# A hybrid attention and gMLP layer on one core: q and k projected by seven products of token halves and k halves

## The chip, the cores and the metric

The kernel runs on one core of a Trainium2 chip. Times are microseconds on the device, from the first to the last instruction of one execution; the metric is the median over repeated runs. Engines: TensorE (PE, with its weight loads PEld), VectorE (DVE), ScalarE (ACT), GpSimd (POOL) and SyncE (SP), which issues most DMAs.

## What is computed

One decoder layer on 512 tokens of width 1024. A single input projection feeds attention (8 heads of 64, rotary on the first 16 dimensions, causal, with blocks of 256 of which all earlier ones are chosen at this size) and a gated spatial mixing (gMLP). Both results are normalised, joined and projected, then come a squared-ReLU MLP of width 4096 and a gated per-layer embedding. All is fp32.

```python
hn = rms_norm(h, mix_pre_g[i])
proj = jnp.einsum('bsd,de->bse', hn, w_in[i])
q, k, v, u, gv = jnp.split(proj, [D_ATTN, 2 * D_ATTN, 3 * D_ATTN, 3 * D_ATTN + D_GMLP], axis=-1)
q = partial_rope(q.reshape(B, S, N_ATTN_HEADS, HEAD_DIM), pos)
k = partial_rope(k.reshape(B, S, N_ATTN_HEADS, HEAD_DIM), pos)
attn_out = moba_attention(q, k, v)
gmlp_out = gmlp_spatial_gating(gelu(u), gelu(gv), ...)
mixed = concatenate([rms_norm(attn_out, ...), rms_norm(gmlp_out, ...)])
h = h + rms_norm(mixed @ w_o[i], mix_post_g[i])
```

## The kernel before

**Split numbers.** Every fp32 matrix is written as a high part (rounded to fp32r by ScalarE) and a low part (the remainder, by VectorE). `product` then does three matmuls into one bank: high by high, high by low, low by high.

**Input projection.** x comes in transposed (`xT_raw`, 16 KB a partition) and is split into `actT_hi` and `actT_lo`. The weights come as slabs of 128 rows by 512 columns; SyncE loads them in pairs into `raw` (four places), ScalarE multiplies by the norm gain and writes `w_hi`, VectorE writes `w_lo` (`splits`). A ring of 16 places holds two groups of eight slabs. A tile `("proj", n)` is 128 tokens by 512 columns: 8 slabs by 3 matmuls, 24 matmuls of 128x512. The groups in order are gv (0 to 3), u (4 to 7), q (8 to 11), k (12 to 15), v (16 to 19); proj 20 to 27 are the output projection.

**Around it.** `normalise` on GpSimd and `ln_centre` on VectorE alternate over the four token tiles of gv: GpSimd computes a root, VectorE centres, GpSimd applies gain and offset. Then GpSimd masks the mixing weights. `mix(i)` does the spatial mixing of two channel groups, `mix_drain(i)` multiplies u by it. q and k tiles are scaled into `work` (two places) by ScalarE, rotated there by GpSimd (`rotate`, five small operations) and transposed by TensorE (`turn_qk`, result `qkT`); ScalarE and VectorE drain the transposes into high and low parts. `turn_gate` does the same with the mixed u. `scores(0)` is the first work of attention, and proj 17 comes behind it.

**Order.** Each engine runs its own list of instructions as the code is written; semaphores are the only link between engines. `phase_one_results` names the order in which banks of PSUM are filled and which bank each result uses; `bank_free` makes TensorE wait until the last user of a bank is drained. SyncE's list is in order as well: a load that waits for its place holds up those behind it. Proj 17 and everything behind it are the same in both kernels, but for places named below.

Of the kernel before, what the change touches and what calls it, by code (L numbers as in the profile page):

```python
# [166 lines left out]
def phase_one_results():  # L167
# [26 lines left out]
    return names[:names.index(("proj", 17))] + [name for name, _ in late], banks  # L194
# [43 lines left out]
EARLY_SPLITS = (KD, KD + 2, KD + 4, KD + 6, KD + 8)  # L238
SPLIT_AT = {n: KD + 2 * (n + 1) for n in range(TT, 16)}


def hymba_layer(nc, x, xT, pT, weights, columns, rope, ws, rows, out):
# [6 lines left out]
    with ExitStack() as ctx:  # L249
# [29 lines left out]
        top[0] = -(-top[0] // (2 * KIB)) * 2 * KIB  # L279
        h = place("h", [P, TT, D])  # L280
# [49 lines left out]

        acc = place("acc", [P, TT, D], at=at_area)
# [11 lines left out]
        at_h = 20 * KIB  # L343
# [49 lines left out]
        rstd_ln = stat[:, 80:84]  # L393
        bn6 = lambda t: stat[:, 90 + 6 * t:96 + 6 * t]
# [28 lines left out]
        roped = sem("roped")  # L423
        gm_squared, gm_rstd, gm_scaled = sem("gm_squared"), sem("gm_rstd"), sem("gm_scaled")
# [73 lines left out]
        drained = {}  # L498

# [87 lines left out]
        def _(dve):  # L587
# [85 lines left out]
            def qkT_lo(i):  # L673

                cut = slice(i % TT * P, (i % TT + 1) * P)
                high, low = ((qT_hi, qT_lo), (kT_hi, kT_lo))[i // TT]
                if i == TT:
                    dve.wait_ge(xT_lo_done, len(X_PIECES))
# [16 lines left out]
            splits(EARLY_SPLITS[4])  # L695
            for n in range(TT, 16):
                if n in SPLIT_AT:
                    splits(SPLIT_AT[n])
                if n in (TT, TT + 1):
                    ln_centre(n - 2)  # L700
                if n in (9, 10):
                    mix_drain(2 * (n - 9))
                    mix_drain(2 * (n - 9) + 1)
                if n >= 10:
                    qkT_lo(n - 10)
                if n == 11:
                    dve.wait_ge(gm_rstd, 1)
                    for t in range(TT):
                        nc.vector.tensor_scalar(u[:, t, :], u[:, t, :], rstd_gm[:, t:t + 1], None,
                                                ALU.mult).then_inc(gm_scaled, 1)  # L710
# [1871 lines left out]
```

## Time and profile before

| what | value |
|---|---|
| median of 3 runs | 590.27 us (589.64 to 590.51) |
| the profiled execution: time, span | 589.68 us, 588.0 us |
| TensorE busy | 579.6 us (99%) |
| VectorE busy | 467.4 us (79%) |
| ScalarE busy | 340.0 us (58%) |
| GpSimd busy | 100.7 us (17%) |
| mean granted clock of TensorE | 0.997 |

Busy shares are means over the whole span. A matmul's record lasts longer than the distance to the next one, since matmuls are pipelined; the pace is read from the distance between starts. In a timeline a row gives the start, the time from there to the end of the last of its instructions, and in brackets how long the engine sat idle before it and what released it.

### The profile page before, as it was taken

What the parts mean: (1) busy time and instruction counts of PE and PEld (TensorE: products, weight loads), DVE (VectorE), ACT (ScalarE), POOL (GpSimd) and SP (SyncE); (2) the same over time, 40 slices, a digit from 0 to 9 for tenths busy, and PEclk for the clock granted to TensorE, in tenths of its full rate; (3) what the DMA queues carried; (4) which work ended last, traced back from release to release, by engine and by line L of the source; (5) the groups of instructions that cost most, each with busy time, mean ns of one, the idle gap of its engine ahead of it and who ended that gap; (6) DMA issues with size and microseconds to landing.
All of it is one profiled execution on the core that took longest, in us unless ns stands there. A gap on an engine that the chain in (4) does not pass through costs nothing.

```text
span 588.0 us, 8944 instructions
## 1 busy us (share of the span) xinstructions
PE 579.6 (99%) x3424; PEld 505.5 (86%) x3424; DVE 467.4 (79%) x623; ACT 340.0 (58%) x555; POOL 100.7 (17%) x159
## 2 busy tenths in 40 slices
PE   9999999999999999999999999999999999999995
PEld 7888888888888878888999989999999999988885
DVE  5655554567866999899999989999999899799655
ACT  6835535657554746676565565764656657654422
POOL 0166333000112445001101010011010100001011
PEclk9999999999999999999999999999999999999998
DMA  8945332112203368649478394583773845584011
GB/s 272 337 130 182 124 107 73 36 64 82 72 1 109 112 246 295 135 112 269 75 226 179 72 268 90 150 245 55 241 168 75 261 96 137 207 292 190 0 73 71
DMA packets 25673, 87.16 MB, mean 148 GB/s; under 512 B 2976, under 2 KB 4384, under 8 KB 25120
## 3 DMA queue, kind: packets, MB, share of 16 engines
q1 hardware_dynamic: 19872, 64.50, 32.3%
q0 software_dynamic: 4032, 14.68, 14.4%
q10 hardware_dynamic: 1728, 7.42, 3.4%
q8 instruction: 27, 0.44, 0.3%
q14 instruction: 14, 0.11, 0.1%
HBM read 80.30 MB, written 6.29 MB: 147 GB/s over the span
## 4 chain that ended last, share of the span: by engine, by line
PE 87%; DVE 5%; DMA 4%; ACT 2%; issue 1%; SPq 0%; POOL 0%; ACTq 0%; DVEq 0%
PE psum L2082 27%; PE psum L2086 27%; PE psum L2087 27%; DMA ple_spill<-ple 2%; PE psum L2137 2%; PE psum L2269 2%; PE psum L2249 1%; DMA raw<-weights_dram 1%; DVE up_lo L832 1%; PE psum L2151 1%; DVE w_lo L600 1%; DMA first_raw_a<-weights_dram 1%; ACT t_hi L1581 1%; DVE raw L957 1%; DVE acc L1032 0%
## 5 line engine op out<-in xcount | busy, mean ns | idle before, releaser
L2082 PE MATMUL psum<-w_hi,actT_hi 128*128 128x512 f32 (+1 forms) x230 | 89.5, 389 | 0.0
L2087 PE MATMUL psum<-w_hi,actT_lo 128*128 128x512 f32 (+1 forms) x230 | 88.0, 383 | 0.0
L2086 PE MATMUL psum<-w_lo,actT_hi 128*128 128x512 f32 (+1 forms) x230 | 87.8, 382 | 0.0
L2082 PE MATMUL psum<-t_hi,a_hi 128*128 128x512 f32 x216 | 84.8, 393 | 0.3 <-DVE acc L1030 0.3
L2086 PE MATMUL psum<-t_lo,a_hi 128*128 128x512 f32 x216 | 84.6, 392 | 0.0
L2087 PE MATMUL psum<-t_hi,a_lo 128*128 128x512 f32 x216 | 84.0, 389 | 0.0
L2087 PE MATMUL psum<-sum_hi,up_lo 128*128 128x256 f32 x224 | 63.4, 283 | 0.0
L2086 PE MATMUL psum<-sum_lo,up_hi 128*128 128x256 f32 x224 | 63.4, 283 | 0.0
L2082 PE MATMUL psum<-sum_hi,up_hi 128*128 128x256 f32 x224 | 63.2, 282 | 0.0
L2087 PE MATMUL psum<-actT_hi,up_lo 128*128 128x256 f32 (+1 forms) x200 | 60.0, 300 | 0.0
L2086 PE MATMUL psum<-actT_lo,up_hi 128*128 128x256 f32 (+1 forms) x200 | 60.0, 300 | 0.0
L2082 PE MATMUL psum<-actT_hi,up_hi 128*128 128x256 f32 (+1 forms) x200 | 59.9, 299 | 0.0
L1903 POOL DMA_DIRECT2D raw_x<-weights_dram x21 | 18.5, 883 | 213.0 <-DVE t_lo L975 212.7
L603 DVE SCALAR_TENSOR_TENSOR w_lo<-raw,cols,w_hi 128x512 fp32r<-128x512 f32 x48 | 38.2, 838 | 18.7 <-ACT w_hi L1234 18.7
L2087 PEld LDWEIGHTS psum<-w_hi,actT_lo 128*128 128x128 f32 x230 | 43.2, 188 | 8.4
L1034 DVE TENSOR_TENSOR acc<-acc,psum 128x512 f32<-128x512 f32 x76 | 49.0, 680 | 1.8 <-PE psum L2087 1.8
L2082 PEld LDWEIGHTS psum<-w_hi,actT_hi 128*128 128x128 f32 x230 | 43.3, 188 | 8.3
L2086 PEld LDWEIGHTS psum<-w_lo,actT_hi 128*128 128x128 f32 x230 | 43.3, 188 | 8.0
L832 DVE TENSOR_TENSOR up_lo<-raw,up_hi 128x1024 fp32r<-128x1024 f32 x37 | 46.7, 1262 | 3.4 <-ACT up_hi L1447 2.8
L2087 PEld LDWEIGHTS psum<-t_hi,a_lo 128*128 128x128 f32 x216 | 40.6, 188 | 8.9
L2082 PEld LDWEIGHTS psum<-t_hi,a_hi 128*128 128x128 f32 x216 | 40.8, 189 | 7.7 <-issue 0.5
L2086 PEld LDWEIGHTS psum<-t_lo,a_hi 128*128 128x128 f32 x216 | 40.7, 189 | 6.6
(229 smaller groups left out, 1337.0 us busy)
## 6 DMA issues: line engine op xcount, KB each, us to landing
raw<-weights_dram SPq DMA_DIRECT2D x42, 512.0 KB, 3.5
raw_o<-weights_dram SPq DMA_DIRECT2D x23, 512.0 KB, 4.4
raw_x<-weights_dram POOLq DMA_DIRECT2D x21, 512.0 KB, 5.6
raw_second<-weights_dram SPq DMA_DIRECT2D x14, 512.0 KB, 4.2
raw_x<-weights_dram SPq DMA_DIRECT2D x9, 512.0 KB, 6.1
gate_raw<-weights_dram SPq DMA_DIRECT2D x8, 512.0 KB, 4.8
raw_o<-weights_dram POOLq DMA_DIRECT2D x7, 512.0 KB, 7.6
h<-x_dram ACTq DMA_DIRECT2D x4, 512.0 KB, 4.8
```

Source lines behind the costliest of these rows:

```text
L600: nc.vector.tensor_tensor(w_lo[:, place_at, :], source, high, ALU.subtract).then_inc(slab_lo, 1)
L603: nc.vector.scalar_tensor_tensor(out=w_lo[:, place_at, :], in0=source, scalar=gain, in1=high, op0=ALU.mult, op1=ALU.subtract).then_inc(sla ...
L832: nc.vector.tensor_tensor(up_lo[q % UP_SLOTS][:], block_source(step, j), up_hi[q % UP_SLOTS][:].bitcast(F32), ALU.subtract).then_inc(block ...
L957: nc.vector.tensor_tensor(target, target, block, ALU.add).then_inc(block_summed, 1)
L1034: nc.vector.tensor_tensor(part, part, bank, how).then_inc(product_added, 1)
L1581: nc.scalar.activation(t_hi[n % T_RING][:], t_source(n), ACT.Copy).then_inc(t_hi_done, 1)
L1903: nc.gpsimd.dma_start(raw_x[step % 2][:], weights[down_in_stream(step, rows, half)], accum_op=ALU.add).then_inc(x_added, 16)
L2082: begin = nc.tensor.matmul(out, a_hi, b_hi, start=first, stop=False, skip_group_check=read_between)
L2086: nc.tensor.matmul(out, a_hi, b_lo, start=False, stop=False, skip_group_check=read_between)
L2087: return nc.tensor.matmul(out, a_lo, b_hi, start=False, stop=last, skip_group_check=read_between)
L2137: mm = nc.tensor.transpose(psum[:, banks[name], j * P:(j + 1) * P], source[:, j * P:(j + 1) * P], ident[:])
L2269: mm = nc.tensor.matmul(psum[s * DH:(s + 1) * DH, BANK_O, pair * P:(pair + 1) * P], v[:, k, head * DH:(head + 1) * DH], probsT_of[place_in ...
```

## The change

q and k are computed together as a 2 by 2 block product. With X the tokens in halves by k in halves (X11, X12; X21, X22) and W the k halves by the columns of q and of k (W11, W12; W21, W22), seven products of sums replace the eight plain ones. A product is two token tiles by four k slabs by three matmuls, 24 matmuls of 128x512. The names BLOCK_21, BLOCK_11, BLOCK_T1, BLOCK_T2, BLOCK_T3, BLOCK_22, BLOCK_T4 give the weight block or sum of each product, in order; SUM_E, SUM_S2, SUM_S3, SUM_S4 are the sums of x halves.

- The four weight blocks are loaded whole (2 DMAs of 512 KB each) into `qk_raw`, gained in place by ScalarE (`qk_gain`, four operations of 128x512 each), and split whole, 128x2048 (`qk_split_hi`, `qk_split_lo`). T1, T2 and T4 are summed in the place of block 11, T3 in that of block 12 (`qk_sum_blocks`).
- The sums of x are made in `xT_raw`, and split into `xs_hi` and `xs_lo`, which lie where x was in `h`. So x is loaded again by SyncE, after product 22.
- Results are put together by ScalarE copies (`qk_copies`) and VectorE (`qk_sum`), with a negated rstd that GpSimd now makes. The q and k tiles come out as q0, q1, k2, k3, k0, k1, q2, q3.
- `mix(0)` and `mix(1)` stand behind product 21, `mix(2)` and `mix(3)` behind product 11, in banks 4 and 7 by turns. proj 16 (v, tile 0) is split around two transposes, and the transposes of q2 and q3 stand behind proj 17.

```diff
+QK_ORDER = ((QK_Q, 0), (QK_Q, 1), (QK_K, 2), (QK_K, 3), (QK_K, 0), (QK_K, 1), (QK_Q, 2), (QK_Q, 3))
...
+    for i in range(4):
+        banks["mix", i] = (BANK_S + 1, BANK_O)[i % 2]
...
+        qk_raw = {BLOCK_21: place("qk_raw_21", [P, 4, W], at=at_second_raw),
+                  BLOCK_11: place("qk_raw_11", [P, 4, W], at=at_area + 16 * KIB),
+                  BLOCK_T3: place("qk_raw_12", [P, 4, W], at=at_mixed_hi),
+                  BLOCK_22: place("qk_raw_22", [P, 4, W], at=at_mixed_lo)}
...
+            def qk_split_lo(j):
+                dve.wait_ge(qk_hi, j + 1)
+                high, low = qk_places(j)
+                nc.vector.tensor_tensor(low, qk_source(j)[:], high.bitcast(F32), ALU.subtract).then_inc(qk_lo, 1)
...
+                nc.vector.tensor_tensor(target[:], target[:], block[:], ALU.add).then_inc(qk_blocks_summed, 1)
...
+            xs_sum(SUM_E, x_block(1, 0), x_block(1, 1), ALU.subtract, 1)
+            ln_centre(2)
+            ln_centre(3)
+            qk_split_lo(BLOCK_21)
...
+            xs_sum(SUM_S4, x_block(0, 1), xs_source(SUM_S2), ALU.add, 4)
+            qk_sum_blocks(BLOCK_T1)
+            xs_split_lo(SUM_S2)
+            qk_split_lo(BLOCK_T1)
+            qk_sum_blocks(BLOCK_T2)
+            qk_split_lo(BLOCK_T2)
+            qk_sum_blocks(BLOCK_T3)
+            mix_drain(0)
+            mix_drain(1)
...
+            nc.gpsimd.tensor_scalar(neg_rstd_x, rstd_x, -1.0, None, ALU.mult).then_inc(x_rstd, 1)
...
+            sp.wait_ge(qk_filled, 2 * BLOCK_22 + 2)
+            for t in range(TT):
+                sp.dma_start(h[:, t, :], x[t * P:(t + 1) * P]).then_inc(x_loaded[t], 16)
...
+            qk_product(BLOCK_21)
+            mix(0)
+            mix(1)
+            qk_product(BLOCK_11)
+            mix(2)
+            mix(3)
+            qk_product(BLOCK_T1)
+            turn_qk(0)
+            turn_qk(1)
+            qk_product(BLOCK_T2)
+            qk_product(BLOCK_T3)
+            turn_gate(0)
+            qk_product(BLOCK_22)
```

VectorE before, from the splits of the last u slabs and the first q slabs (`w_lo`) with the centrings (`gv`) to the drains of the mixing groups (`u`):

```order
L603 SCALAR_TENSOR_TENSOR w_lo<-raw,cols,w_hi 128x512 [waits slab_hi] x4
L655 TENSOR_SCALAR gv<-gv,stat 128x512 [waits ln_rstd]
L603 SCALAR_TENSOR_TENSOR w_lo<-raw,cols,w_hi 128x512 [waits slab_hi] x2
L655 TENSOR_SCALAR gv<-gv,stat 128x512 [waits ln_rstd]
L603 SCALAR_TENSOR_TENSOR w_lo<-raw,cols,w_hi 128x512 [waits slab_hi] x8
L668 SCALAR_TENSOR_TENSOR u<-psum,cols,u 128x4x64 [waits act_drained,filled]
L668 SCALAR_TENSOR_TENSOR u<-psum,cols,u 128x4x64
L668 SCALAR_TENSOR_TENSOR u<-psum,cols,u 128x4x64 [waits filled]
L668 SCALAR_TENSOR_TENSOR u<-psum,cols,u 128x4x64
```

VectorE after, from the sum E to the same drains (`qk_raw_91` is block 21, `_92` block 11 and the sums in its place, `_93` block 12, `_94` block 22; `xs_lo_97` and `_98` are the two places of x sums):

```order
L729 TENSOR_TENSOR xT_raw<-xT_raw 128x2x512
L699 TENSOR_SCALAR gv<-gv,stat 128x512 [waits ln_rstd,xs_summed]
L699 TENSOR_SCALAR gv<-gv,stat 128x512 [waits ln_rstd]
L740 TENSOR_TENSOR w_lo<-qk_raw_91,w_hi 128x2048 [waits qk_hi]
L729 TENSOR_TENSOR xT_raw<-xT_raw 128x2x512
L729 TENSOR_TENSOR xT_raw<-xT_raw 128x2x512 [waits xs_summed]
```

and a little further on:

```order
L751 TENSOR_TENSOR qk_raw_92<-qk_raw_92,qk_raw_93 128x2048 [waits qk_gained,qk_lo,xs_summed]
L734 TENSOR_TENSOR xs_lo_98<-xT_raw,xs_hi_96 128x1024 [waits xs_hi_done]
L740 TENSOR_TENSOR w_lo<-qk_raw_92,w_hi 128x2048 [waits qk_hi]
L751 TENSOR_TENSOR qk_raw_92<-qk_raw_92,qk_raw_94 128x2048 [waits qk_gained,qk_lo]
L740 TENSOR_TENSOR w_lo<-qk_raw_92,w_hi 128x2048 [waits qk_hi]
L751 TENSOR_TENSOR qk_raw_93<-qk_raw_93,qk_raw_94 128x2048 [waits qk_gained,qk_blocks_summed]
L712 SCALAR_TENSOR_TENSOR u<-psum,cols,u 128x4x64 [waits act_drained,filled]
L712 SCALAR_TENSOR_TENSOR u<-psum,cols,u 128x4x64
L712 SCALAR_TENSOR_TENSOR u<-psum,cols,u 128x4x64 [waits filled]
L712 SCALAR_TENSOR_TENSOR u<-psum,cols,u 128x4x64
L740 TENSOR_TENSOR w_lo<-qk_raw_93,w_hi 128x2048 [waits qk_hi]
L760 SCALAR_TENSOR_TENSOR work<-psum,stat,work 128x512 [waits qk_filled,qk_copied] x2
```

The drains of mixing groups 0 and 1 stood behind plain splits; now they stand behind the block sums and low parts of T1 and T2 and the sum T3, each with a wait for ScalarE's high part, and no split is left between the centrings.

ScalarE before, from the drain of the second u tile (`u`) with the splits around it to the drain of the first q tile (`work`):

```order
L1307 ACTIVATE u<-psum,stat 128x512 [waits filled]
L1234 ACTIVATE w_hi<-raw,cols 128x512 [waits slab_used,raw_loaded1]
L1234 ACTIVATE w_hi<-raw,cols 128x512
L1349 DMA rope_sb<-rope_dram 128x128
L1307 ACTIVATE u<-psum,stat 128x512 [waits filled]
L1234 ACTIVATE w_hi<-raw,cols 128x512 [waits slab_used,raw_loaded0]
L1234 ACTIVATE w_hi<-raw,cols 128x512
L1307 ACTIVATE u<-psum,stat 128x512 [waits filled]
L1234 ACTIVATE w_hi<-raw,cols 128x512 [waits slab_used,raw_loaded1]
L1234 ACTIVATE w_hi<-raw,cols 128x512
L1312 ACTIVATE work<-psum,stat 128x512 [waits filled]
```

ScalarE after, from the drain of the u tile of proj 6 on (`work` now holds the copies of product 21):

```order
L1436 ACTIVATE u<-psum,stat 128x512 [waits filled]
L1451 ACTIVATE qk_raw_94<-qk_raw_94,cols 128x512 [waits qk_raw_loaded3]
L1451 ACTIVATE qk_raw_94<-qk_raw_94,cols 128x512 x3
L1464 ACTIVATE w_hi<-qk_raw_92 128x2048 [waits slab_used,qk_blocks_summed]
L1436 ACTIVATE u<-psum,stat 128x512 [waits filled]
L1464 ACTIVATE w_hi<-qk_raw_92 128x2048 [waits slab_used,qk_blocks_summed]
L1485 ACTIVATE work<-psum,stat 128x512 [waits qk_filled] x2
L1464 ACTIVATE w_hi<-qk_raw_93 128x2048 [waits qk_filled,qk_blocks_summed]
L1464 ACTIVATE w_hi<-qk_raw_94 128x2048 [waits qk_filled,qk_gained]
```

The drain of the last u tile, proj 7, has moved behind the high part of T1, and the copies of product 21 behind that of T2.

TensorE at mixing groups 2 and 3, before and then after (L2371 is `mix`, `xs_hi` marks product T1):

```order
L2151 MATMUL psum<-gv,wsT 128x256 [waits dve_drained]
L2151 MATMUL psum<-gv,wsT 128x256
L2151 MATMUL psum<-gv,wsT 128x256 [waits dve_drained]
L2151 MATMUL psum<-gv,wsT 128x256
L2137 MATMUL psum<-ident,work 128x128 [waits act_drained,roped]
```

```order
L2371 MATMUL psum<-gv,wsT 128x256 [waits dve_drained]
L2371 MATMUL psum<-gv,wsT 128x256
L2371 MATMUL psum<-gv,wsT 128x256 [waits dve_drained]
L2371 MATMUL psum<-gv,wsT 128x256
L2302 MATMUL psum<-w_hi,xs_hi_95 128x512 [waits qk_copied,xs_lo_done,qk_lo]
```

In both, groups 2 and 3 wait for VectorE to drain groups 0 and 1. Behind them stood the first transpose; now there is product T1, which waits for the copies of product 21, the low part of E and the low part of T1.

## Rows read from the trace of the kernel before

**Rows 1.** the page: busy times, and the clock in 40 slices

```profile
PE 579.6 (99%) x3424; PEld 505.5 (86%) x3424; DVE 467.4 (79%) x623; ACT 340.0 (58%) x555; POOL 100.7 (17%) x159
...
PEclk9999999999999999999999999999999999999998
```

**Rows 2.** the page: the chain that ended last, by engine

```profile
PE 87%; DVE 5%; DMA 4%; ACT 2%; issue 1%; SPq 0%; POOL 0%; ACTq 0%; DVEq 0%
```

**Rows 3.** timeline of TensorE: start us, us, engine, line, tiles, count

```profile
54.70 1.89 PE L2151 MATMUL psum<-gv,wsT 128*128 128x256 f32 x8
...
56.24 0.58 PE L2082 MATMUL psum<-w_hi,actT_hi 128*128 128x512 f32 x1
...
57.80 0.39 PE L2082 MATMUL psum<-w_hi,actT_hi 128*128 128x512 f32 x1
...
61.66 0.39 PE L2087 MATMUL psum<-w_hi,actT_lo 128*128 128x512 f32 x1
...
106.77 0.60 PE L2137 MATMUL psum<-ident,work 128*128 128x128 f32 x4
...
107.30 0.34 PE L2082 MATMUL psum<-kT_hi,mixT_hi 64*128 64x128 f32 x2
...
108.80 0.50 PE L2082 MATMUL psum<-w_hi,actT_hi 128*128 128x512 f32 x1
```

**Rows 4.** groups by form, VectorE: shapes, count, busy us, mean ns, idle before

```profile
L832 DVE TENSOR_TENSOR up_lo<-raw_second,up_hi 128x1024 fp32r<-128x1024 f32 x14 | 17.1, 1221 | 1.2 <-ACT up_hi L1447 0.5
...
L981 DVE TENSOR_TENSOR a_lo<-f,a_hi 128x512 fp32r<-128x512 f32 x28 | 19.1, 682 | 0.4 <-ACT a_hi L1592 0.4
...
L603 DVE SCALAR_TENSOR_TENSOR w_lo<-first_raw_b,cols,w_hi 128x512 fp32r<-128x512 f32 x4 | 2.8, 749 | 0.7 <-ACT w_hi L1234 0.7
```

**Rows 5.** timeline of ScalarE at 36.90

```profile
36.90 2.55 ACT L1234 ACTIVATE w_hi<-raw,cols 128x512 fp32r<-128x512 f32 x4
```

**Rows 6.** groups by form, ScalarE

```profile
L1447 ACT ACTIVATE up_hi<-raw_second 128x1024 fp32r<-128x1024 f32 x14 | 14.7, 1048 | 0.0
```

**Rows 7.** timeline of VectorE, 18 to 62

```profile
18.12 1.41 DVE L603 SCALAR_TENSOR_TENSOR w_lo<-raw,cols,w_hi 128x512 fp32r<-128x512 f32 x2 [0.70 <-ACT w_hi L1234]
...
29.05 2.44 DVE L603 SCALAR_TENSOR_TENSOR w_lo<-raw,cols,w_hi 128x512 fp32r<-128x512 f32 x2
...
48.03 0.55 DVE L655 TENSOR_SCALAR gv<-gv,stat 128x512 f32<-128x512 f32 x1 [0.44 <-POOL stat L1799]
...
59.85 1.65 DVE L668 SCALAR_TENSOR_TENSOR u<-psum,cols,u 128x256 f32<-128x256 f32 x4
```

**Rows 8.** timeline of GpSimd, 29 to 84

```profile
29.31 1.64 POOL L1819 TENSOR_TENSOR gv<-gv,ln_gb 128x512 f32<-128x512 f32 x1 [1.74 <-DVE gv L655]
...
37.92 1.29 POOL L1819 TENSOR_TENSOR gv<-gv,ln_gb 128x512 f32<-128x512 f32 x1 [0.72 <-DVE gv L655]
...
52.07 1.09 POOL L1832 TENSOR_SCALAR_AFFINE_SELECT wsT<-wsT 128x1024 f32<-128x1024 f32 x1
...
83.50 0.32 POOL L1848 TENSOR_TENSOR work<-rope_tmp 128x64 f32<-128x64 f32 x1
...
83.79 0.83 POOL L1850 TENSOR_TENSOR work<-rope_tmp 128x64 f32<-128x64 f32 x1
```

**Rows 9.** the page: DMA issues, KB, us to landing

```profile
raw<-weights_dram SPq DMA_DIRECT2D x42, 512.0 KB, 3.5
```

**Rows 10.** timeline of VectorE at the first scores

```profile
108.18 0.69 DVE L621 TENSOR_TENSOR kT_lo<-psum,kT_hi 128x512 fp32r<-128x512 f32 x1 [4.78 <-ACT kT_hi L1253]
...
108.92 1.23 DVE L722 TENSOR_TENSOR psum<-psum,causal 128x1024 f32<-128x1024 f32 x1
```

**Rows 11.** timeline of TensorE, the first turned probabilities

```profile
115.73 1.03 PE L2249 MATMUL psum<-ident,probs 128*128 128x128 f32 x8
```

**Rows 12.** windows at the end: TensorE busy (x), PEclk, DMA

```profile
581.00:582.00 1.00, 0.84 (x8) 0.63 (x6) 0.00 (x0) 0.12 (x1) 0.85 (x2) 1.00 0.00 0
...
585.00:585.50 0.50, 0.00 (x0) 0.00 (x0) 0.47 (x2) 0.00 (x0) 0.00 (x0) 0.50 0.00 0
```

More of the change, by code:

```diff
@@ L673, in qkT_lo @@
             def qkT_lo(i):
[L675 to L678, printed above, removed]
+                which, t = QK_ORDER[i]
+                cut = slice(t * P, (t + 1) * P)
+                high, low = ((qT_hi, qT_lo), (kT_hi, kT_lo))[which]
                 turn_lo(("qkT", i), low[:, :, cut], high[:, :, cut], bank1["qkT", i])
@@ L694, in _ @@
             ln_stats_of(3)
[L695 to L710, printed above, removed]
-                if 12 <= n <= 15:
-                    gate_turn_lo(n - 12)
@@ L716, in row_maxima @@
+            qkT_lo(2)
+            qkT_lo(3)
+            qk_sum(4)
+            qk_sum(5)
+            gate_turn_lo(1)
+            splits(G_V * KD + 4)
+            splits(G_V * KD + 6)
+            gate_turn_lo(2)
+            qkT_lo(4)
+            qkT_lo(5)
+            gate_turn_lo(3)
+            splits(G_O0 * KD)
             def row_maxima(unit):
@@ L1307, in proj_drain @@
                     last = nc.scalar.activation(u[:, t, :], bank, ACT.Gelu, scale=rstd)
-                elif group in (G_Q, G_K):
-                    i = n - 2 * TT
-                    if i >= 2:
-                        act.wait_ge(filled, filled1["qkT", i - 2])
-                    last = nc.scalar.activation(work[:, i % 2, :], bank, ACT.Copy, scale=rstd)
                 else:
@@ new lines, in _ @@
+            proj_drain(7)
+            qk_split_hi(BLOCK_T2)
+            qk_copies(BLOCK_21)
+            qk_split_hi(BLOCK_T3)
+            qk_split_hi(BLOCK_22)
+            act.wait_ge(*drained["mix", 3])
+            for t in range(TT):
+                square(u[:, t, :], ss_gm[:, t:t + 1], gm_squared)
+            qk_copies(BLOCK_T1)
+            qkT_hi(0)
+            qkT_hi(1)
+            xs_split_hi(SUM_S3)
+            qk_split_hi(BLOCK_T4)
+            qk_copies(BLOCK_T2)
+            xs_split_hi(SUM_S4)
@@ L1364, in _ @@
+            gate_turn_hi(0)
+            splits(G_V * KD)
+            splits(G_V * KD + 2)
+            qkT_hi(2)
+            qkT_hi(3)
+            gate_turn_hi(1)
+            splits(G_V * KD + 4)
+            splits(G_V * KD + 6)
+            qk_scale(6)
+            qk_scale(7)
+            gate_turn_hi(2)
+            act.wait_ge(qk_summed, 6)
+            act.dma_start(gain_post[:], rows["mix_post"]).then_inc(post_loaded, 16)
+            qkT_hi(4)
+            qkT_hi(5)
             proj_drain(16)
-            qkT_hi(7)
+            gate_turn_hi(3)
@@ L2224, in scores @@
+            proj(16, range(0, 4))
+            turn_qk(4)
+            turn_qk(5)
+            proj(16, range(4, KD))
+            turn_gate(3)
             def scores(unit):
```

309 lines of the change are left out of this document (239 added, 70 removed).

## The prediction

> **What bounds the kernel now.** I read the page's busy times and clock first [rows 1]: TensorE is busy for 99% of the span and its granted clock reads 9 (90% or more) in every slice but the last. The chain that ended last [rows 2] gives 87% to TensorE, 5% to VectorE and 4% to DMA. Then I read the stretch that changes in order of time [rows 3]. From the products of u to the first scores TensorE never stops: 18 matmuls lie between the starts at 57.80 and 61.66, less one, so 17 steps take 3.86 us, 0.227 each; a tile of 24 takes 5.45. The mixing block begins at 54.70, which is where the first q tile ends, so the u products end at 54.70 - 5.45 = 49.25. The v tile that follows the first scores (proj 17) starts at 108.80. The stretch is 59.55 us long and TensorE alone fills it. So a matmul less is worth 0.227 us, if its operands are there in time, and any wait of TensorE here goes straight to the end.
>
> **What the change takes away.** q and k took 8 tiles of 24 matmuls, now 7 products of 24: 5.45 us. Two transpose groups (qkT 6 and 7) go behind proj 17; one group takes 107.30 - 106.77 = 0.53 or less [rows 3], I take 0.48, so 0.96 leaves the stretch and comes back behind it.
>
> **What it adds.** On VectorE, 16 splits of 128x512 go (0.75 each [rows 4], 0.66 start to start). In come 4 sums of x halves and 4 low parts of them (128x1024), 4 sums of weight blocks and 7 low parts of blocks (128x2048), and 6 sums of results (128x512). A 1024-wide one takes 1.22 us and a 512-wide one 0.68 [rows 4], so 0.54 more for each further 512: 2048 wide is 2.30, and 2.26 start to start; 1024 is 1.14. That is 11 x 2.26 + 8 x 1.14 + 6 x 0.65 = 37.9 us for 10.6. On ScalarE, gaining four blocks is 16 x 0.64 (four take 2.55 [rows 5]); a 1024-wide copy is 1.05 [rows 6], so a 2048-wide is about 1.9, and 1.8 start to start. Each block has to go ScalarE (high), VectorE (low), VectorE (sum onto it), ScalarE (high) and so on, because T1 and T2 are summed in the place of block 11. That is the chain to follow.
>
> **The schedule, by these durations.** VectorE's fourth centring waited for GpSimd until 48.03 [rows 7] with splits just before it. Now the splits in front of it are gone, and it runs at about 47.5; VectorE can do nothing in between, since it stands ahead of the first low part. The low part of block 21 runs 47.9 to 50.2. TensorE was ready at 49.25: **wait 1.1**.
> GpSimd's last normalising (two operations of 1.3, each 1.29 when alone) and its mask of the mixing weights (1.09) come now [rows 8]. In the trace two splits next to such an operation took 2.44 in place of 1.41 [rows 7], and GpSimd's 1.64 in place of 1.29 [rows 8]: 29.31 + 1.64 = 30.95, and one more split after that ends at 31.5, just what one operation after another gives. So I let operations of VectorE with two inputs in SBUF and operations of GpSimd take turns, 3.6 us for VectorE here. The sums for S3 and S2 end at 55.0 and the low part of 11 at 58.3. TensorE has finished 21 and two mixing groups (56.24 - 54.70 = 1.54 [rows 3]) at 57.3: **wait 1.2**.
> Low part of E, sum S4, block sum T1 end at 63.0. ScalarE makes T1's high part until 64.9, and only behind it drains proj 7 (65.6), whose bank the second half of product 11 needs at 61.2: **wait 4.5**.
> Low T1 to 67.4, sum T2 to 69.8, high T2 on ScalarE to 71.7, low T2 to 74.1, sum T3 to 76.4, and then the drains of mixing groups 0 and 1 (four operations take 1.65 [rows 7], 0.83 a group). Mixing group 2 now reuses the bank of group 0, so TensorE, ready at 68.4, starts it at 77.3: **wait 8.9**.
> T1 runs 79.0 to 84.4. The two rotations on GpSimd begin at 81.5, while VectorE goes from mixing drains to the sum T4 and the low part of 22, 2.26 each. A small GpSimd operation took 0.83 in place of 0.32 next to one split of 0.75 [rows 8]; the second rotation gets one of its five operations in between each long one and ends at 89.2. TensorE has done the first transpose at 84.9: **wait 4.4**.
> T2 starts at 89.8; behind it I find no wait over 0.1 us up to proj 17: T3's x part is ready when T2 ends, and the v slabs (loads 3.5 us [rows 9]) and blocks are in time. The second load of x is 4 transfers on SyncE's queue when product 22 is done (about 105). It is wanted some 40 us later, and even if they land one after another, 14 us, the w_o slabs queued behind them land by 122.5 and are wanted at 123: 0. The negated rstd costs GpSimd 0.3 before it joins the first wait.
> Waits: 1.1 + 1.2 + 4.5 + 8.9 + 4.4 = 20.1. Proj 17 starts at 108.80 - 5.45 - 0.96 + 20.1 = 122.5, 13.7 later.
>
> **Behind it.** The transposes come back: +0.96. Before, the row maxima of the first scores began 0.12 after proj 17 (108.92) [rows 10]. Now a gate low part and two splits stand ahead of them on VectorE, 2.1 us behind proj 17, and two low parts stand ahead of the drain of the turned probabilities. TensorE turned the probabilities at 115.73 with 1.3 in hand [rows 11]; by the same arithmetic it now waits 1.2 for the inverse, 1.3 for the drain and 1.0 in the next group, 3.5 in all. The bounds are 0 (the cover that attention had, used up differently) and 3.5; I take 2.0. After that TensorE is as full as before and nothing gives the time back. **Sum: 13.7 + 1.0 + 2.0 = 16.7.** The profiled execution took 589.68 (span 588.0), so 606.4 by it; the median of the three runs is 0.6 higher, 590.27, so **607.0**.
>
> **Taking turns, or not.** The turn-taking above is read off the rows: 2.44 for 1.41. The Trainium skill ("SBUF — State Buffer", section "Who interferes with whom") says that an instruction of VectorE with two SBUF inputs and one of GpSimd that reads SBUF exclude each other, the first one keeping the ports to its end. The trace agrees, with 30.95 and 31.5. Without it the sum is that of the first rival.
>
> **The rivals.**
> 1. GpSimd hinders the long operations little (they overlap as far as they like). Then the waits are 2.3 (proj 7), 8.9 (mixing) and 2.3 (T3's x part), 13.5 together, and the sum 13.5 - 6.4 + 3.0 = 10.1: 600.4. The 8.9 stays, since no GpSimd work lies beside it. Against it: rows 7 and 8. Chance 0.17.
> 2. Clock. In the trace TensorE's last matmuls are in 581:582, at a clock of 1.00, and in 585:585.5, after 3 us without one, it reads 0.50 [rows 12]. A wait of 8.9 us outlasts that, and T1 would start at 1.2 GHz. If all 24 matmuls of T1 ran at twice 0.227 that is 5.45 more, but the wait of 4.4 behind T1 takes up most: +1. If T2 were slow too, +5.5 more: 612. Chance 0.08. The Trainium skill ("TensorE: Matmul & The Clock Gate", section "HAM oscillation — how this bites in real kernels") says that a long gap drops the clock again; the trace agrees on the fall at its end and shows no recovery inside the kernel.
> 3. The shift is partly taken back in attention and the layers after it, or the small waits are hidden: only the 8.9 and 2.3 at full size, and the rest half. 8.9 + 2.3 + 2.2 + 1.2 - 6.4 + 1.0 = 9.2: 599.5. For it: VectorE has gaps in this stretch, as the 4.78 before 108.18 [rows 10]. Chance 0.12.
> 4. Faster than before. One mechanism: the 2048-wide operations run at a higher rate than the shorter ones. The point from which it decides is about 0.6 us each on VectorE with 0.8 on ScalarE: then the waits before proj 17 are 2.3 and it starts 4.2 earlier; with all of the 3.5 behind it hidden, 1.0 of transposes back, the time is 587. Against it: 512 and 1024 wide are in proportion in the trace (0.68, 1.22). Chance 0.03.
> Forecast 0.60.
>
> **The numbers.** The likeliest case itself spans 14 to 19 more (2048 wide at 2.15 or 2.35 moves it by 1.4 either way, attention 0 or 3.5): 604 to 610. The range takes in rivals 1 to 3 up to their middles, for a chance left out of 2 in 10: 598 to 612. Within 0.2% (1.2 us, what a measurement of this kernel can tell from no change) lies only an accident between rivals 3 and 4: 0.02. Faster 0.03, slower 0.95.
>
> **What the profile will show.** TensorE busy falls from 99% to about 96%, with idle ahead of the mixing matmuls released by VectorE's u operations (near 68 to 77), ahead of a w_hi product released by ScalarE's u drain (near 61 to 66) and ahead of a transpose released by GpSimd (near 85 to 89). The 2048-wide operations read 2.3 (VectorE) and 1.9 (ScalarE). Proj 17 starts near 122. I am wrong if the drains of mixing groups 0 and 1 come before 70, if the long operations are shorter than 1.6, or if the second rotation ends less than 3 us after the first.

## The result, and the profile after

The changed kernel takes 605.14 us (median of 4 runs, 605.03 to 605.33), the kernel before 590.07 beside it on the same chip (589.64 to 590.51): a ratio of 1.0256, 95% interval 1.0238 to 1.0273. It is slower by 15.1 us; 16.7 were forecast, to 607.0. The profiled executions differ as much: span 603.1 against 588.0.

The page of the kernel after, busy times and slices, to be read beside [rows 1]:

```profile
span 603.1 us, 8912 instructions
...
PE 580.3 (96%) x3400; PEld 504.7 (84%) x3400; DVE 494.5 (82%) x632; ACT 356.8 (59%) x566; POOL 107.5 (18%) x160
...
PE   9999389999999999999999999999999999999995
...
DVE  5638887577867699799999999989999999789655
...
PEclk9999779999999999999999999999999999999999
...
PE 70%; DVE 12%; DMA 5%; ACT 5%; POOL 4%; issue 2%; SPq 1%; ACTq 0%; DVEq 0%; POOLq 0%
```

TensorE has a hole in the fifth and sixth slices (60 to 90 us), its clock falls in the same two, and the chain that ended last has lost 17 points of TensorE to the other engines [rows 2]. The timeline of TensorE from 49 to 122 us, cut to the steps that the prediction names, and at the end projection 17 (compare [rows 3]):

```profile
50.60 0.50 PE L2302 MATMUL psum<-w_hi,actT_hi 128*128 128x512 f32 x1 [0.68 <-DVE w_lo L740]
...
56.18 1.89 PE L2371 MATMUL psum<-gv,wsT 128*128 128x256 f32 x8
...
58.17 0.50 PE L2302 MATMUL psum<-w_hi,actT_hi 128*128 128x512 f32 x1
...
65.29 0.79 PE L2302 MATMUL psum<-w_hi,actT_hi 128*128 128x512 f32 x1 [4.10 <-ACT u L1436]
...
69.37 0.40 PE L2307 MATMUL psum<-w_hi,actT_lo 128*128 128x512 f32 x1
...
76.63 3.78 PE L2371 MATMUL psum<-gv,wsT 128*128 128x256 f32 x8 [6.86 <-DVE u L712]
79.85 0.99 PE L2302 MATMUL psum<-w_hi,xs_hi 128*128 128x512 f32 x1
...
86.58 0.60 PE L2357 MATMUL psum<-ident,work 128*128 128x128 f32 x4
...
88.48 0.66 PE L2357 MATMUL psum<-ident,work 128*128 128x128 f32 x4 [1.30 <-POOL work L2051]
...
121.47 0.51 PE L2302 MATMUL psum<-w_hi,actT_hi 128*128 128x512 f32 x1
```

The three longer waits are the three large ones of the forecast, each by the engine it named: ScalarE's drain of projection 7 (L1436) ahead of the second half of product 11, VectorE's drains of mix 0 and 1 (L712) ahead of mix 2, GpSimd's rotation (L2051) ahead of the second turn. Projection 17 starts 12.67 later than in [rows 3] (121.47 for 108.80).

ScalarE at the first of these waits: the high part of T1, and behind it the drain of projection 7.

```profile
62.75 1.91 ACT L1464 ACTIVATE w_hi<-qk_raw 128x2048 fp32r<-128x2048 f32 x1 [3.60 <-DVE qk_raw L751]
64.57 0.67 ACT L1436 ACTIVATE u<-psum,stat 128x512 f32<-128x512 f32 x1
```

VectorE and GpSimd in the same stretch, from their timelines (compare [rows 7, 8]):

```profile
48.26 2.29 DVE L740 TENSOR_TENSOR w_lo<-qk_raw,w_hi 128x2048 fp32r<-128x2048 f32 x1
50.46 4.56 DVE L729 TENSOR_TENSOR xT_raw<-xT_raw 128x1024 f32<-128x1024 f32 x2
55.05 3.07 DVE L740 TENSOR_TENSOR w_lo<-qk_raw,w_hi 128x2048 fp32r<-128x2048 f32 x1
...
75.70 1.66 DVE L712 SCALAR_TENSOR_TENSOR u<-psum,cols,u 128x256 f32<-128x256 f32 x4
```
```profile
48.49 3.21 POOL L2019 TENSOR_TENSOR gv<-gv,ln_gb 128x512 f32<-128x512 f32 x1 [0.73 <-DVE gv L699]
...
82.64 0.46 POOL L2046 TENSOR_TENSOR rope_tmp<-work,rope_sb 128x128 f32<-128x128 f32 x1
83.06 2.37 POOL L2047 TENSOR_TENSOR rope_tmp<-work,rope_sb 128x64 f32<-128x64 f32 x1
85.39 2.37 POOL L2048 TENSOR_TENSOR rope_tmp<-work,rope_sb 128x64 f32<-128x64 f32 x1
```

A 2048-wide operation takes 2.29 alone and 3.07 beside GpSimd; GpSimd's operation of 1.29 takes 3.21, and its operation of 0.32 takes 2.37 when a long one of VectorE has just begun. The clock, from the windows (columns: stretch, length, busy of PE, PEld, DVE, ACT, POOL, granted clock, DMA):

```profile
61.00:65.00 4.00, 0.19 (x1) 0.00 (x0) 3.16 (x3) 2.25 (x2) 0.00 (x0) 1.00 0.00 0
65.00:68.00 3.00, 2.71 (x6) 2.15 (x7) 2.97 (x2) 0.24 (x1) 0.00 (x0) 0.50 0.00 0
68.00:70.00 2.00, 1.76 (x7) 1.08 (x5) 1.31 (x1) 0.65 (x1) 0.00 (x0) 0.89 0.00 0
...
76.00:80.00 4.00, 3.37 (x9) 2.75 (x9) 3.59 (x6) 3.53 (x2) 0.00 (x0) 0.50 0.00 0
80.00:83.00 3.00, 3.00 (x10) 2.35 (x10) 3.00 (x8) 0.02 (x1) 1.98 (x6) 0.65 0.00 0
83.00:86.00 3.00, 3.00 (x15) 2.47 (x14) 3.00 (x2) 2.90 (x9) 3.00 (x3) 1.00 0.00 0
```

Already the wait of 4.1 us leaves TensorE at 0.50, 1.2 GHz, for most of the second half of product 11. After the wait of 6.9 all of the mixing and the first four matmuls of T1 run at it (a matmul then takes 0.43 us from start to start in place of 0.23).

### The profile page after: what moved, and what is told of

It is laid out like the page before. It is cut to its first block, busy times and chain, and to the rows that moved or that the text cites. A ratio compares the mean times of both kernels' runs of the same rounds, so it can differ in the third digit from the quotient of the medians.

```text
span 603.1 us, 8912 instructions
## 1 busy us (share of the span) xinstructions
PE 580.3 (96%) x3400; PEld 504.7 (84%) x3400; DVE 494.5 (82%) x632; ACT 356.8 (59%) x566; POOL 107.5 (18%) x160
## 4 chain that ended last, share of the span: by engine, by line
PE 70%; DVE 12%; DMA 5%; ACT 5%; POOL 4%; issue 2%; SPq 1%; ACTq 0%; DVEq 0%; POOLq 0%
PE psum L2302 22%; PE psum L2306 22%; PE psum L2307 22%; DMA ple_spill<-ple 2%; DMA raw<-weights_dram 2%; DVE up_lo L956 2%; PE psum L2541 2%; PE psum L2357 1%; PE psum L2521 1%; DVE w_lo L740 1%; DVE qk_raw L751 1%; DMA first_raw_b<-weights_dram 1%; ACT w_hi L1464 1%; DVE xT_raw L729 1%; DVE w_lo L647 1%
## 5 line engine op out<-in xcount | busy, mean ns | idle before, releaser
L2302 PE MATMUL psum<-w_hi,actT_hi 128*128 128x512 f32 (+1 forms) x190 | 74.4, 392 | 4.9 <-ACT u L1436 4.1
L2307 PE MATMUL psum<-w_hi,actT_lo 128*128 128x512 f32 (+1 forms) x190 | 72.9, 383 | 0.0
L2306 PE MATMUL psum<-w_lo,actT_hi 128*128 128x512 f32 (+1 forms) x190 | 72.8, 383 | 0.0
L2302 PEld LDWEIGHTS psum<-w_hi,actT_hi 128*128 128x128 f32 x190 | 36.1, 190 | 12.9 <-ACT u L1436 4.5
L2302 PEld LDWEIGHTS psum<-sum_hi,up_hi 128*128 128x128 f32 x224 | 42.9, 191 | 1.1
L2306 PEld LDWEIGHTS psum<-sum_lo,up_hi 128*128 128x128 f32 x224 | 42.9, 191 | 1.1
L2307 PEld LDWEIGHTS psum<-sum_hi,up_lo 128*128 128x128 f32 x224 | 42.9, 191 | 0.0
```

The costliest lines, as they stand in the source:

```text
L2302: begin = nc.tensor.matmul(out, a_hi, b_hi, start=first, stop=False, skip_group_check=read_between)
L2306: nc.tensor.matmul(out, a_hi, b_lo, start=False, stop=False, skip_group_check=read_between)
L2307: return nc.tensor.matmul(out, a_lo, b_hi, start=False, stop=last, skip_group_check=read_between)
```

## The experiments

All start from the changed kernel; runs 8 to 10 change the order of much of it. Each ratio is to the kernel before on the same chip; the changed kernel's is 1.0256. Theory A and theory B are those of the text on record ahead of each run.

**1. The drain of projection 7 first.** On ScalarE:

```diff
+            proj_drain(7)
             qk_split_hi(BLOCK_T1)
-            proj_drain(7)
```

> Only the order on ScalarE changes: the drain of projection 7 comes ahead of the high part of T1, so that the second half of product 11 no longer waits for it (4.1 us in the kernel after the change). Theory A, VectorE's row of long operations from 48 to 78 us sets when mix 2 may begin, whatever TensorE does before: the 4.1 us go over to the wait ahead of mix 2, which grows from 6.9 to about 11 us and still ends at 76.6, and the time stays within 0.5 us of 605.1. Theory B, each wait of TensorE is a cost of its own: the 4.1 us are saved, 601.0.

604.97 us, ratio 1.0255 (1.0241 to 1.0269). From its list of TensorE's steps:

```profile
76.61 3.78 PE L2371 MATMUL psum<-gv,wsT 128*128 128x256 f32 x8 [12.68 <-DVE u L712]
```

Theory A: 4.1 us are taken from one wait and stand in the next, with the 1.6 us that the half product no longer loses to the low clock, and that wait ends where it did (76.61 for 76.63). TensorE's waits here are not costs that add up; VectorE's row of operations sets the end.

**2. The drains of mix 0 and 1 first.** As 1, and on VectorE:

```diff
             xs_split_lo(SUM_S2)
+            mix_drain(0)
+            mix_drain(1)
             qk_split_lo(BLOCK_T1)
             ...
-            mix_drain(0)
-            mix_drain(1)
```

> As the run before, and on VectorE the drains of mix 0 and 1 come ahead of the low part of T1 in place of behind the sum of T3. Mix 2 then starts some 12 us sooner, at about 65. Theory A (VectorE's amount of work up to the rotated queries is the bound, not its order): what was won is lost again ahead of product T1 (the copies of product 21 and the low part of T1) and ahead of the two turns of the queries; the first turn is at 86 to 88 as before, and the time is 605 to 606.5. Theory B (the order of VectorE's work is at fault): the 6.9 us ahead of mix 2 are saved for the most part, 599 or less.

608.08 us, ratio 1.0314 (1.0300 to 1.0328). TensorE's three large waits in it, and the window behind the last:

```profile
72.44 0.77 PE L2302 MATMUL psum<-w_hi,xs_hi 128*128 128x512 f32 x1 [5.92 <-ACT work L1485]
...
83.06 0.66 PE L2357 MATMUL psum<-ident,work 128*128 128x128 f32 x4 [2.56 <-POOL work L2051]
...
88.92 1.12 PE L2357 MATMUL psum<-ident,work 128*128 128x128 f32 x4 [5.21 <-POOL work L2051]
```
```profile
89.00:95.00 6.00, 6.00 (x18) 4.86 (x19) 4.71 (x8) 3.34 (x3) 1.18 (x2) 0.54 0.02 4
```

Mix 2 starts at 64.5, 12 us sooner, and the second turn no sooner (88.92 for 88.48). That is theory A, but I missed the size by 1.6 us or more: the last wait is now 5.2 us, and the first 11 matmuls of product T2 behind it run at half speed (the mean clock from 89 to 95 is 0.54), so that T2 takes 7.8 us in place of 5.45. A wait that moves takes the drop of the clock with it, to a place where nothing covers it. That the order does not count holds for this exchange only: runs 8 to 10 put work before 48 us, and there it does.

**3. The two waits filled with work.** On TensorE, behind each half of product 11:

```diff
+                    if b == BLOCK_11:
+                        for _ in range((66, 115)[j]):
+                            nc.tensor.matmul(psum[:, BANK_PT, 0:P], warm[:], warm[:], start=True, stop=True)
```

> TensorE gets work that nobody needs in its two long waits: 66 matmuls of 128x128 behind the first half of product 11 and 115 behind the second half, at 0.053 us each at the full clock 3.5 and 6.1 us, a little less than the waits of 4.1 and 6.9 us. If idling is what lets the granted clock fall, it stays at 1.00 from 61 to 86 us, mixing takes 1.6 us in place of 3.2 and product T1 5.45 in place of 6.7. Theory A (behind product T1 stands the second rotation, which ends at 88.4 whatever the clock): the time stays within 0.4 us of 605.1, and the wait ahead of the second turn grows from 1.3 to about 4 us. Theory B (the lower clock costs its full length): 2.5 to 3 us less, about 602.3.

606.64 us (604.76 to 606.71, 5 runs), ratio 1.0273 (1.0258 to 1.0287), 1.1 us above what theory A allowed. The clock is 1.00 from 61 to 84.7 us and T1 ends at 84.1, 2.45 sooner; the second turn is at 88.65:

```profile
88.65 1.07 PE L2357 MATMUL psum<-ident,work 128*128 128x128 f32 x4 [3.93 <-POOL work L2051]
```

Theory B falls. Theory A has the mechanism, and again I left out what follows: after 3.9 us idle T2 begins at half speed and takes 1.4 us longer. That is the profiled execution, one of three that took 606.6 to 606.7; the other two took 604.8 and 605.0, and no trace shows the clock in them. In the changed kernel the slow T1 covered this wait.

**4. Two long operations cut in four.** VectorE's sum of T4 (shown) and low part of 22 (cut likewise):

```diff
+                if j == BLOCK_T4:
+                    for k in range(4):
+                        last = nc.vector.tensor_tensor(target[:, k], target[:, k], block[:, k], ALU.add)
+                    last.then_inc(qk_blocks_summed, 1)
+                    return
                 nc.vector.tensor_tensor(target[:], target[:], block[:], ALU.add).then_inc(qk_blocks_summed, 1)
```

> VectorE's sum of T4 and low part of 22, each one operation of 2048 elements a row (2.39 and 2.41 us), are cut into four of 512 each, the same work. Theory A (GpSimd waits for the end of one VectorE operation at a time): its two small products of the second rotation, 2.37 us each behind the long ones, take under 0.9 us each, the second rotation ends by 86.0 in place of 88.4, the second turn follows the first without the wait of 1.3 us, and the time falls by 0.6 to 1.3 us, to about 604.1; VectorE itself takes about 0.5 us longer over the two. Theory B (GpSimd is held off as long as VectorE has such work queued): nothing changes, the rotation ends at 88.4 or later and the time is 605.1 to 605.6.

602.44 us, ratio 1.0220 (1.0206 to 1.0234), 2.1 us below the changed kernel by the ratios. GpSimd's second rotation:

```profile
82.56 0.77 POOL L2058 TENSOR_TENSOR rope_tmp<-work,rope_sb 128x64 f32<-128x64 f32 x1
83.29 0.76 POOL L2059 TENSOR_TENSOR rope_tmp<-work,rope_sb 128x64 f32<-128x64 f32 x1
```

0.77 for 2.37: GpSimd waits here for the end of one operation of VectorE, and the length of that one is its price. Theory A. I had the gain at 1.3 at most. Both turns run in one piece from 85.26, and product T2 starts at 86.05 in place of 88.89. Of that 1.4 is the wait, 0.5 the lead that this execution had at 50 us already, which is no gain of the edit, and 0.8 a T1 that was back at the full clock at 80 us and not at 82. That too lies ahead of the first operation that the edit changes (82.3), but without the wait behind T1 it counts, and with the wait it would not have.

**5. Three block sums cut to 8 columns.** The sums of T1, T2 and T3 leave out the other 504 columns; every wait stays.

```diff
+                n = W if j == BLOCK_T4 else 8
-                nc.vector.tensor_tensor(target[:], target[:], block[:], ALU.add).then_inc(qk_blocks_summed, 1)
+                nc.vector.tensor_tensor(target[:, :, 0:n], target[:, :, 0:n], block[:, :, 0:n], ALU.add
+                                        ).then_inc(qk_blocks_summed, 1)
```

> The sums of blocks T1, T2 and T3 are cut to 8 of the 512 columns (the rest of the three blocks keeps what stood there, so the projected q and k are wrong in them); every wait stays. Each sum then takes about 0.1 us in place of 2.29. Theory A (the row high part on ScalarE, low part on VectorE, sum on VectorE, repeated for T1 and T2, sets when mix 2 may begin): mix 2 begins about 6.5 us sooner, at 70, the second turn of the queries as much sooner, and the time is 598 to 600. Theory B (the waits come from the order of TensorE's own steps, or from GpSimd): the time stays above 603.

598.50 us, ratio 1.0149 (1.0135 to 1.0164). Mix 2 starts at 70.18 and the second turn at 82.03, both 6.45 sooner:

```profile
70.18 3.78 PE L2373 MATMUL psum<-gv,wsT 128*128 128x256 f32 x8 [4.10 <-DVE u L712]
...
82.03 0.66 PE L2359 MATMUL psum<-ident,work 128*128 128x128 f32 x4 [0.97 <-POOL work L2053]
```

Three operations of 2.2 us on VectorE (6.6 together) are 6.3 us of the whole time by the ratios, 6.6 by the medians: this row is the bound, nearly one to one. Theory A.

**6 and 7. A product cut from 24 matmuls to 4**, T1 in the one, T4 in the other:

```diff
-                    for k in range(4):
+                    for k in range(0, 4, 3 if b == BLOCK_T1 else 1):
+                        if b == BLOCK_T1:
+                            mm = nc.tensor.matmul(psum[:, first_bank + j, :], x_high, w_high[:, k, :], ...)
+                            continue
```

> Product T1 takes 4 matmuls in place of 24 (its result is not the product then), nothing else changes. It ran at the lower clock for the most part and took 6.73 us; the 20 that are left out are 5.6 us of that. Theory A (behind it the second rotation sets the pace): the first turn comes at about 82.6, the second still waits until 88.4, and nothing is saved; as TensorE has then idled for longer, product T2 may begin at the lower clock, so 605 to 608. Theory B (a product saved is worth its length): 5.6 us less, 599.5.

607.31 us, ratio 1.0294 (1.0281 to 1.0307).

```profile
88.48 1.12 PE L2357 MATMUL psum<-ident,work 128*128 128x128 f32 x4 [5.20 <-POOL work L2051]
```

> Product T4, which in the kernel after the change begins and ends with no wait of TensorE beside it (107.1 to 112.6 us), takes 4 matmuls in place of 24 (its result is not the product then). The 20 are 4.54 us at the full clock. Theory A (VectorE's and GpSimd's steps for the keys, the queries and the splits for v stand close behind TensorE here too): the turn of the fifth tile waits for GpSimd's rotation, which ends at 114.4 whatever TensorE does, and 1 to 2.5 us are saved, 602.6 to 604. Theory B (here TensorE alone sets the pace, so a product is worth its length): 4.5 us less, 600.6.

603.76 us (602.07 to 604.35), ratio 1.0231 (1.0218 to 1.0244).

```profile
110.18 0.63 PE L2357 MATMUL psum<-ident,u 128*128 128x128 f32 x4 [2.21 <-DVE mixT_lo L665]
...
112.85 0.63 PE L2302 MATMUL psum<-w_hi,actT_hi 128*128 128x512 f32 x1
...
115.00 1.03 PE L2357 MATMUL psum<-ident,work 128*128 128x128 f32 x8
```

Twenty matmuls less make the kernel 2 us slower at T1 (the second turn at 88.48 as ever, then T2 at the low clock) and 1.5 us faster, not 4.5, at T4. So even T4, which ran without a wait beside it, is worth only a third of its length in this kernel. The trace shows where its 4.5 us go, and it is not the rotation of theory A: TensorE stands idle for 2.2 us until VectorE has written the low part of the turned gate, and the half product behind that runs mostly at the low clock, 4.4 us for 2.85. The turn at 115.00 waits for nothing and is 0.8 us sooner than in the changed kernel.

**8. The early order.** Block 11's gain and the token sums go into idle time before 48 us. The heart of VectorE's list (more calls change place further back, and ScalarE's in step):

```diff
             splits(EARLY_SPLITS[1])
+            xs_sum(SUM_E, ...)
+            xs_sum(SUM_S3, ...)
+            xs_sum(SUM_S2, ...)
             ln_stats_of(0)
             ...
             qk_split_lo(BLOCK_21)
-            xs_sum(SUM_S3, ...)
-            xs_sum(SUM_S2, ...)
             qk_split_lo(BLOCK_11)
-            xs_split_lo(SUM_E)
-            xs_sum(SUM_S4, ...)
             qk_sum_blocks(BLOCK_T1)
             xs_split_lo(SUM_S2)
+            qk_sum_blocks(BLOCK_T3)
+            qk_sum(0)
             qk_split_lo(BLOCK_T1)
-            qk_sum_blocks(BLOCK_T2)
-            qk_split_lo(BLOCK_T2)
-            qk_sum_blocks(BLOCK_T3)
             mix_drain(0)
             mix_drain(1)
```

> The whole computation, with the steps of VectorE and ScalarE in another order: the token sums E, S3 and S2 go to VectorE's idle time at 22 to 25.4 us and S4 to 32, the gain of block 11 to before that of 21, the drains 4 to 7 and the copies of product 21 come sooner, VectorE takes the low part of 11 right behind that of 21, then the sum of T1, the sum of T3, the first scaled sum of the queries, the low part of T1 and the drains of mix 0 and 1, and further back the rotations' inputs stand ahead of the low parts that nobody waits for yet. Theory A (the 24 matmuls are saved; what the change lost is VectorE's and ScalarE's row of steps, much of which can lie in idle time that they have before 48 us): the waits of TensorE shrink to 2 to 6 us and the time is 584 to 592. Theory B (the amount of work on VectorE between 48 and 97 us, with GpSimd in turns, is too much in any order): above 597.

Neither theory as it stood: of 12 executions four took 589.92 to 590.95 and eight 598.26 to 600.87 (the median of all is 599.61); the ratio of the four is 1.0037 (1.0005 to 1.0068). The profiled one is of the eight. Its one long wait, and GpSimd's and VectorE's timelines at that time:

```profile
81.30 1.11 PE L2366 MATMUL psum<-ident,work 128*128 128x128 f32 x4 [7.41 <-POOL work L2060]
```
```profile
70.81 0.32 POOL L2058 TENSOR_TENSOR work<-rope_tmp 128x64 f32<-128x64 f32 x1
71.09 10.16 POOL L2060 TENSOR_TENSOR work<-rope_tmp 128x64 f32<-128x64 f32 x1
```
```profile
71.05 4.48 DVE L740 TENSOR_TENSOR w_lo<-qk_raw,w_hi 128x2048 fp32r<-128x2048 f32 x2
75.45 2.28 DVE L751 TENSOR_TENSOR qk_raw<-qk_raw,qk_raw 128x2048 f32<-128x2048 f32 x1
77.65 1.22 DVE L734 TENSOR_TENSOR xs_lo<-xT_raw,xs_hi 128x1024 fp32r<-128x1024 f32 x1
78.79 2.28 DVE L740 TENSOR_TENSOR w_lo<-qk_raw,w_hi 128x2048 fp32r<-128x2048 f32 x1
```

A step of 0.32 us came 0.04 us behind the start of a long one and got its turn only when five of them were over. They run at 2.28, the length of one that nobody disturbs: here the two engines did not take turns at all. The wait of 7.4 and a T2 that then takes 7.8 us in place of 5.45 make 9.8, about what lies between the two groups of times. No trace of one of the four is there; that they lack the long step is concluded from run 9.

**9. The same with a guard.**

```diff
             mix_drain(3)
+            dve.wait_ge(roped, 2)
             qk_split_lo(BLOCK_T2)
```

> The run with the early order, and one wait more: VectorE waits for the end of GpSimd's second rotation before it begins the low part of T2. In the profiled execution of the early order the last small step of that rotation began at 71.09 us and took 10.16 us, under five long VectorE operations that followed one another without a gap; the second turn waited 7.4 us for it, and of 12 executions eight took 598 to 601 us and four 590 to 591. Theory A (GpSimd gets no turn while VectorE's long operations follow without a gap, by chance in each execution): every execution is now at 589 to 591 us, and the step takes under 1 us. Theory B (the two times have another cause, such as TensorE's granted clock): the times stay spread over 590 to 601.

590.90 us, all 11 executions within 588.43 to 592.07, ratio 1.0013 (1.0002 to 1.0023).

```profile
72.91 0.32 POOL L2061 TENSOR_TENSOR work<-rope_tmp 128x64 f32<-128x64 f32 x1
```

The step takes 0.32, both turns run without a wait, and the times near 600 are gone, with one wait that costs VectorE 0.31 us. Theory A. The spread is wider than I wrote, and the clock goes with it: the three executions with a mean granted clock of 0.994 or 0.995 took 591.5 to 592.1, the eight from 0.997 up 588.4 to 591.2. In the profiled one (591.54) the clock reads 0.50 from 59 to 61 us, behind 1.87 us idle ahead of mix 0.

**10. The third order**, with product 11 split around the first mixing groups:

```diff
+            qk_product(BLOCK_11, (0,))
             mix(0)
             mix(1)
-            qk_product(BLOCK_11)
+            qk_product(BLOCK_11, (1,))
```

> The whole computation in a third order: as the early order, and TensorE takes the first half of product 11 ahead of mix 0 and 1, VectorE takes the low part of block 11 ahead of that of 21, the low part of T1 ahead of the first scaled sum of the queries, and operations that read PSUM (which leave GpSimd alone) stand behind the sums that feed the rotations. Theory A (nearly all waits of TensorE before projection 17 can be ordered away, so that the 24 matmuls, 5.45 us, are won): 583 to 588 us, in every execution alike. Theory B (waits only move, as when the mix drains came first): 590 or more.

588.22 us (587.42 to 588.83, 7 runs), ratio 0.9970 (0.9960 to 0.9981): faster than the kernel before by 0.3%, and than the changed one by 2.8%. I had 588 as the upper end, so theory A in kind and 0.2 us short in size. TensorE's waits from 25 us to the first attention, all of them:

```profile
50.16 0.50 PE L2311 MATMUL psum<-w_hi,actT_hi 128*128 128x512 f32 x1 [0.47 <-DVE w_lo L740]
...
59.45 1.97 PE L2380 MATMUL psum<-gv,wsT 128*128 128x256 f32 x8 [0.84 <-ACT u L1442]
...
116.65 1.09 PE L2551 MATMUL psum<-probsT,v 128*64 128x128 f32 x16 [1.34 <-DVE probsT L866]
```

1.3 us before projection 17 in place of 13; then attention takes back part of the gain. The step of units 1 and 2 starts at 130.24, against 132.10 before: 1.9 us are left of the 5.45.

**11. x loaded a third time.**

```diff
+            for turn in range(2):
                 for t in range(TT):
+                    if turn:
+                        sp.wait_ge(x_loaded[t], 32)
                     sp.dma_start(h[:, t, :], x[t * P:(t + 1) * P]).then_inc(x_loaded[t], 16)
```

> Between the four second loads of x and the next weight loads on the same queue, x is loaded once more over itself (4 loads of 512 KB; each waits for the one before it on the same rows). Theory A (the second load is hidden behind projections whose weights are there already): one more of it costs 0 to 0.5 us, 605.1 to 605.6. Theory B (the loads of v's and the output's weights stand in line behind it): 2 to 5 us more, 607 to 610.

606.60 us (606.10 to 611.14), ratio 1.0300 (1.0276 to 1.0323): 1.5 to 2.6 us more (by the medians, by the ratios), above theory A's 0.5 and at the foot of theory B's 2 to 5. TensorE's steps agree up to 127 us, but ScalarE waits for the output's weights,

```profile
122.11 1.34 ACT L1360 ACTIVATE w_hi<-raw,cols 128x512 fp32r<-128x512 f32 x2 [1.26 <-DMA raw<-weights_dram]
```

and the first attention starts at 134.51 for 133.13. In the changed kernel this operation waited for no load (120.71). So the second load of x is hidden as forecast, but its cover is less than one more of it.

## Why the prediction was right, and where it was not

| step | forecast | measured |
| --- | --- | --- |
| 24 matmuls, two turns moved | -5.45, -0.96 | as forecast |
| TensorE ready for 21 | 49.25 | 49.76, 0.5 later |
| wait for the low part of 21 | 1.1 | 0.84 (49.76 to 50.60) |
| wait for the low part of 11 | 1.2 | 0.45 (58.17 - 56.18, less the 1.54 of [rows 3]) |
| drain of projection 7, second half of 11 starts | 65.7, wait 4.5 | 65.29, wait 4.4 |
| mix 2 starts | 77.3, wait 8.9 | 76.63, wait 7.0 |
| second rotation done, second turn | 89.2, wait 4.4 | 88.43, wait 1.4 |
| low clock: half of 11, mixing, T1 | 0 | 1.6 + 1.7 + 1.3 = 4.6 |
| projection 17 starts | +13.7 | +12.67 |
| attention, to the step of units 1 and 2 | +1.0 +2.0 | +1.95 in all (146.72 - 132.10 = 14.6) |
| whole | +16.7 | +15.1 |

The waits are by starts here, with TensorE's work in between at full speed, so each is a little more than the profile's idle figure. The 0.5 us, the waits and the low clock are 19.2 together; less 5.45 and 0.96 that is 12.8, within 0.1 of the 12.67.

**The row of VectorE, ScalarE and GpSimd** was the right thing to follow, and its lengths were right: 2.29 for 2048 wide (2.30 forecast; 2.20 from start to start, forecast 2.26), 1.91 on ScalarE, and the taking of turns at 48 to 58 and 83 to 88 us. Three of its events, 65.3, 76.6 and 88.4, came within 0.8 us of the forecast. Runs 1 and 5 show that it is the cause: the end does not move when TensorE's wait of 4.1 us is taken away, and moves nearly one to one with VectorE's sums.

**The waits as separate terms** were the weak form of a right sum. The forecast added five waits with TensorE at full speed. Two of them came out 1.9 and 3.0 short, and 4.6 us of slow matmuls stand in their place. Rival 2 had said this of T1 and given it a chance of 0.08; it happened, earlier than that rival had it (after 4.1 us), and cost nothing, because the next event of VectorE or GpSimd fixed the time anyway. Run 3, with the clock held up, was not faster, and its second turn stood where it had (88.65 for 88.48). "T2 too", its dear half, did not happen here, and did in runs 2, 3, 6 and 8. The chance for a fallen clock was too small and its prices too high. The rival let all 24 matmuls of a product run at half speed, and the clock came back inside each: T1 lost 1.3 us, not 5.45, all of it covered where the rival had +1, and T2 lost 1.4 us in run 3 and 2.4 in runs 2, 6 and 8, not 5.5. Its 612 is a slip as well, since 607.0 and 1 and 5.5 are 613.5. The rule that the prediction quoted from the Trainium skill ("TensorE: Matmul & The Clock Gate", section "HAM oscillation — how this bites in real kernels"), that a long gap drops the clock again, held after both long waits (0.50 in 65:68 and in 76:80). The recovery, which no row of before could show, is in the windows 68:70 (0.89) and 83:86 (1.00).

**Attention** was sized at +3.0 and took 1.95: the transposes, and one wait of 0.98 for the drain of the turned probabilities in place of three. VectorE began the first scores 1.3 us behind projection 17 (122.80), not 2.1.

**The first rival** (GpSimd hinders little) is refuted by the 3.21 and 2.37 and by run 4. **The third** (part is taken back) was right in one term: attention took one wait of three. **The fourth** is refuted by 2.29.

**The second load of x** at 0: right, with less in reserve than the text has it. It put the output's weights at 122.5 and their use at 123; run 11, where the next weight load behind x is issued at 115.88 in place of 111.85, shows that a shift of some 4 us is more than there is.

What stays open: why GpSimd got its turn between two long operations at 85.3 us in the profile of the changed kernel, and none at four such borders in run 8; and why the clock fell behind 1.9 us idle in run 9's trace and not behind the same 1.9 us in run 8's. The 0.5 us by which the profiled executions' ends differ beyond attention (15.1 against 14.6) is no open term: from the step of units 1 and 2 to the end the 13 profiled kernels take 455.5 to 456.6 us, the one before 455.9 and the changed one 456.4.

## What to carry to other kernels

Fewer matmuls help only where their operands are ready; price such an exchange as a row of events on the engines that prepare them, and read TensorE's waits as the difference to that row, not as terms that add. A wait removed from TensorE alone turns up at the next such event, and may end in front of work that then runs at the low clock. Preparation belongs in those engines' idle time before the stretch. Where small GpSimd steps stand beside a row of VectorE operations on SBUF, cut the long ones (run 4) or let VectorE wait for the step (run 9).

## What the runs showed of the hardware that was not expected

- A GpSimd operation with SBUF operands can be starved: 10.16 us for a step of 0.32, behind five operations of VectorE on SBUF with no gap between them, in the profiled execution of run 8; the times say that it comes in some executions of one kernel and not in others. In other places the two took turns after each operation. The Trainium skill ("SBUF — State Buffer", section "Who interferes with whom") states the exclusion; that the turn may not come was seen only here.
- Filling TensorE's waits with matmuls kept the granted clock at 1.00 for 24 us and made three of five executions slower; in the profiled one the idle time had moved to a place ahead of T2.
- A wait of 4.1 us was enough: the granted clock was 0.50 when TensorE began again, and 0.89 in 68:70. Shorter ones were not all alike: behind 1.30 us idle it stayed at 1.00 (the second turn of the changed kernel), behind 2.2 us it fell to a mean of 0.59 in 112:115 (run 7), and behind 1.9 us it fell to 0.50 in 59:61 in one trace (run 9) and stayed at 1.00 in another (run 8).
